# A two-layer mixer and a sparse-attention block on one NeuronCore: in the attention steps of the grouped heads, the first run of the next scores is issued between the first and the second group of turned blocks

## What is computed

```python
def block_attention(q, k, v):        # q (B,S,H,D), k (B,T,G,D), v (B,T,G,Dv)
    ...
    def one_block(qi):               # 128 queries
        s = jnp.einsum('bqgrd,bkgd->bgrqk', qi, k).astype(jnp.float32) * scale
        p = jax.nn.softmax(s, axis=-1).astype(v.dtype)
        return jnp.einsum('bgrqk,bkgv->bqgrv', p, v)
```

## Time and profile before

| | us |
|---|---|
| median of 3 runs | 4646.46 |
| the runs | 4642.58 to 4646.97 |
| span of the profiled execution | 4643.8 |
| PE busy | 4460.8 (96%) |
| DVE busy | 2440.1 (53%) |
| ACT busy | 1280.8 (28%) |

### The profile page before, as it was taken

The page is one execution under the profiler, slowest core; times in us unless marked ns, Lnnn a source line. Parts: engine busy times, 40 slices in busy tenths (PEclk is TensorE's granted clock), DMA queues, the critical chain, the costliest instruction groups (busy, mean ns, idle before and its releaser), DMA issues.

```text
span 4643.8 us, 46448 instructions
## 1 busy us (share of the span) xinstructions
PE 4460.8 (96%) x18996; PEld 2406.2 (52%) x18996; DVE 2440.1 (53%) x4042; ACT 1280.8 (28%) x2014; POOL 51.9 (1%) x74
## 2 busy tenths in 40 slices
PE   7998999999998999999999999999999999999997
PEld 3554666645444666544457645555544444444443
DVE  6677556633476566326962312333543555556554
ACT  2004444513015445223012402333300311110033
POOL 1000000000000000000000000000000000000000
PEclk9999999999999999999999999999999999999998
DMA  7212000021121000200111010000012211111111
GB/s 278 79 54 86 1 1 1 1 104 59 37 81 38 1 1 1 76 27 24 37 37 32 23 32 23 14 19 15 26 39 68 68 46 36 46 45 64 46 50 68
DMA packets 49458, 207.12 MB, mean 45 GB/s; under 512 B 4896, under 2 KB 4896, under 8 KB 46688
## 3 DMA queue, kind: packets, MB, share of 16 engines
q1 hardware_dynamic: 36512, 142.62, 9.3%
q0 software_dynamic: 12736, 61.54, 3.5%
HBM read 185.27 MB, written 18.87 MB: 44 GB/s over the span
## 4 chain that ended last, share of the span: by engine, by line
PE 91%; DVE 5%; ACT 3%; issue 1%; DMA 1%; POOL 0%; ACTq 0%; DVEq 0%; PEld 0%; PEldq 0%; SPq 0%; POOLq 0%
PE psum L2399 20%; PE psum L703 9%; PE psum L1240 7%; PE psum L1418 5%; PE psum L2079 5%; PE psum L1268 5%; PE psum L1670 5%; PE psum L1254 4%; PE psum L399 3%; PE psum L2353 3%; PE psum L1783 2%; PE psum L1773 2%; PE psum L2365 2%; PE psum L2095 2%; PE psum L1810 2%; PE psum L712 1%
## 5 line engine op out<-in xcount | busy, mean ns | idle before, releaser
L2399 PE MATMUL psum<-arena 128*128 128x512 f32 x2184 | 937.9, 592 | 0.9 <-DVEq L382 0.9
L2399 PEld LDWEIGHTS psum<-arena 128*128 128x128 f32 x2184 | 414.8, 190 | 523.2 <-issue 521.9
L703 PE MATMUL psum<-arena 128*128 128x512 f32 x952 | 410.0, 592 | 0.0
L2704 DVE TENSOR_TENSOR arena<-arena,psum 128x512 f32<-128x512 f32 x280 | 192.5, 688 | 397.1 <-PE psum L2399 388.5
L1240 PE MATMUL psum<-arena 64*128 64x512 f32 (+3 forms) x1200 | 382.9, 531 | 7.4 <-ACT arena L1195 5.8
L1337 DVE TENSOR_REDUCE arena<-psum 128x1 f32<-128x1280 f32 (+1 forms) x216 | 290.8, 1368 | 116.6 <-PE psum L1240 116.6
L1254 PE MATMUL psum<-arena 128*128 128x128 f32 x1968 | 299.9, 279 | 28.1 <-ACT arena L1311 12.8
L1254 PEld LDWEIGHTS psum<-arena 128*128 128x128 f32 x1968 | 225.9, 141 | 173.4 <-issue 110.4
L703 PEld LDWEIGHTS psum<-arena 128*128 128x128 f32 x952 | 180.9, 190 | 223.8 <-issue 222.2
L1306 ACT ACTIVATE arena<-psum,arena 128x1280 f32<-128x1280 f32 (+1 forms) x216 | 265.0, 1232 | 110.5 <-DVE arena L1337 110.4
L1311 ACT ACTIVATE arena<-psum 128x512 f32<-128x512 f32 x294 | 170.1, 596 | 327.4 <-PE psum L1254 327.2
(11 more groups left out here) (293 smaller groups left out, 5105.7 us busy)
## 6 DMA issues: line engine op xcount, KB each, us to landing
arena<-stream SPq DMA_DIRECT2D x228, 512.0 KB, 3.7
arena<-mod_t POOLq DMA_DIRECT2D x32, 512.0 KB, 4.7
arena<-mod_w POOLq DMA_DIRECT2D x4, 2048.0 KB, 26.2
arena<-stream SPq DMA_DIRECT2D x6, 1024.0 KB, 10.4
arena<-x SPq DMA_DIRECT2D x4, 1280.0 KB, 16.6
gated<-arena POOLq DMA_DIRECT2D x4, 1280.0 KB, 4.7
arena<-gated SPq DMA_DIRECT2D x1, 5120.0 KB, 15.8
arena<-x POOLq DMA_DIRECT2D x2, 2048.0 KB, 19.5
```

What stands on the lines that cost most here:

```text
L703: last = nc.tensor.matmul(ps(PROJECT_BANKS[p], 512), lhsT=lhsT(k), rhs=rhs(k), start=k == 0, stop=k == 3)
L2399: last = nc.tensor.matmul(ps(pair_bank(j, p), HALF), lhsT=lhsT(k), rhs=rhs(k), start=k == 0, stop=k == nk - 1)
L2704: step(nc.vector.tensor_tensor(out, a, b, op), ev)
```

## The change

The loop of PE's queue takes the first run of scores of the next step out of the list and issues it between group 0 and group 1, wherever `turns_first` holds; the other runs stay behind group 1.

```diff
             first = turns_first(steps, u)
-            for g in range(min(first, len(groups))):
+            if first:
+                turn(u, 0, groups[0])
+                if ahead:
+                    scores(u + 1, ahead.pop(0))
+            for g in range(1, min(first, len(groups))):
                 turn(u, g, groups[g])
             for i in range(max(len(ahead), len(groups))):
```

## The result

| | before | after |
|---|---|---|
| median, us | 4644.53 | 4656.2 |
| runs | 4642.48 to 4646.97 (7) | 4651.09 to 4660.48 (7) |
| span of the profiled execution, us | 4643.8 | 4655.3 |
| ratio to before | | 1.0023 (95%: 1.0013 to 1.0034) |

The changed kernel is slower by 0.23%: 11.7 us between the medians, 11.5 us between the profiled spans. The forecast was 4659.2 us, 12.7 us above the median of before as it stood then. A second set of runs, beside other kernels, gave 12.9 us between the medians and a ratio of 1.0031 (1.0021 to 1.0042).

A forecast was written before the change was run, and what follows sets the result against it. PE's closed gqa-step loop, with a 0.36 us hole waiting for DVE's L1358, was taken as the bound. Terms 11.2 + 0.6 + 0.1 + 0.9 = 12.8, rounded to + 12.7, on 4646.46 gave 4659.2 us; range 4648 to 4667.

The forecast's parts named there:

- The total: Whole kernel: + 12.7 us on the median of 4646.46 us, giving 4659.2 us; chance 0.74.
- What bounds the step: Gqa steps: PE's closed loop of 8.20 us, with a 0.36 us hole ahead of group 1 waiting for DVE's bank 7 reading.
- New start, + 0.04 us: Gqa steps: half 1's score waits for its exponential and starts at 806.72, 0.04 us later than group 1 did.
- Second entry, + 0.21 us: Gqa steps: scores cut in two pay one more entry (0.11 us) and exit (0.10 us) before group 2.
- The tail of 5.25 us: Gqa steps: from group 2 to the end of half 1's next exponential, 5.25 us, within a new loop of 8.45 us.
- The mla places: Layer 0: group 1 falls behind the score, 0.44 us twice, + 0.9 us; layer 1: 0, at best - 0.2 us.
- The first gqa step of layer 0: Turned blocks at half the spacing there; group 2 comes later, estimate + 0.6 us, between 0 and 1.
- The rest of the kernel should stay as it was: Outside the touched places: no change expected; a longer part elsewhere would make the sum wrong.
- No price for an entry: Rival, gqa places: PE loads the other kind's weights during the last pass; only + 3.4 us, 4649.9 us; chance 0.12.
- The hole filled after all: Rival, gqa steps: half 1's exponential ends earlier, second entry free, up to 0.36 us a step saved, 4631 us; chance 0.04.
- Half 1 waits for half 0: Rival, first score run: half 1 starts only once half 0 is through; + 0.88 us a step, 4688 us; chance 0.10.
- What would show it: Profile after: 8.45 us gqa step, first scores waiting for ACT L1306, no L1358 wait, two score-load rows with 0.54 us first passes.

The follow-up runs named there:

- x6: Kernel before, gqa places only: first two score runs issued between groups 0 and 1, the last between groups 2 and 3; ratio 0.9984 to the kernel before.

## Why the prediction was right, point by point

- **The total.** 12.7 us forecast, 11.7 measured. The prediction's own parts add up to 12.8, or to 12.6 with its 0.244 us a step, for which it gives no source; neither is 12.7.
- **What bounds the step.** Right: in the old order the hole is DVE's reading of bank 7 (7.88 us with a shorter one, 8.20 with a shorter exponential).
- **New start, + 0.04 us.** Right in kind. The exponential of half 1 ends at 805.44 + 0.21 = 805.65 and group 1 starts at 806.75, 1.10 us later; the prediction had 0.05 + 1.07 = 1.12.
- **Second entry, + 0.21 us.** Right for the stretch from the exponential to group 2: group 1 to the second entry 0.59 us, the other two runs 807.34 to 808.83 = 1.49 us, both as worked out. It is not the whole price: on PE's own loop a second entry and exit cost 0.34 us, with the slower spacing of group 0. PE's own loop of 8.22 us was seen when the exponential was made shorter.
- **The tail of 5.25 us.** 808.83 to 813.88 + 0.21 = 814.09 is 5.26 us. The sum of the step, 8.45, was 0.02 us high; 45 x 0.233 = 10.5 us instead of 11.2.
- **The mla places.** Layer 0: 0.43 us each at equal clock, as forecast; in the trace the second is 2.12 us longer, 1.69 of it from the lower clock shown above. Layer 1: 0.06 us each gained.
- **The first gqa step of layer 0.** The term that was mis-sized: 0.6 us forecast, 2.3 us measured from group 0 to group 2. The granted clock was lower there than before. The windows of that piece in after and in before (us, busy times by engine, PEclk, DMA share, GB/s):

```profile
750.40:757.80 7.40, 7.30 (x20) 3.12 (x20) 2.41 (x7) 1.44 (x3) 0.00 (x0) 0.60 0.01 2
```

```profile
747.20:752.20 5.00, 4.95 (x20) 2.98 (x20) 2.26 (x7) 1.39 (x2) 0.00 (x0) 0.66 0.01 3
```

  Both have the same 20 matmul records. In after the half clock (1.2 GHz) also covered the two other runs of scores. At full clock (1.00 granted) the piece took 4.53 us in the changed order with the shorter reading and 3.44 us in the order of before with the shorter exponential. So the order itself costs about 1.1 us here, an estimate across two kernels that differ a little, and the clock the rest. Whether the low clock belongs to the new order is not settled. The second trace of the changed kernel has it again (7.25 us from group 0 to group 2), so has the run with the gqa places alone, and a shorter stretch of it lies in the kernel before. The two shortened kernels in the changed order, at 1.00, do not have it.
- **The rest of the kernel should stay as it was.** It did not, and here luck helped. The stretch between the two layers' attention, in which nothing was changed, is 3.0 us shorter, at a higher granted clock (before, then after):

```profile
960.18:1471.83 511.65, 486.56 (x1279) 234.94 (x1276) 258.51 (x295) 112.43 (x138) 14.68 (x14) 0.98 0.20 72
971.40:1480.04 508.64, 483.52 (x1279) 233.77 (x1276) 258.47 (x295) 112.31 (x138) 14.69 (x14) 0.99 0.20 72
```

  The stretch ahead of the attention is 0.7 us longer and the one behind it 2.0 us shorter. The touched parts together grew by 15.8 us (gqa steps 10.5, the first of them 2.8, mla places 2.4, the last of layer 0 0.1), the untouched ones shrank by 4.3, which leaves the 11.5. At equal clock the touched parts come to about 12.4 us, near the 12.8 of the sum. So the mechanism and its size are shown by the traces; that the total came within 1 us is in part the half clock's moving about.
- **The rivals.** No price for an entry: fell, with the 1.49 us. The hole filled after all: fell for this order, since the exponentials did not move ahead; x6 shows that another order fills part of it. Half 1 waits for half 0: fell. In the first gqa step of layer 0 the halves can be seen apart:

```profile
751.08 0.29 PEld L1240 LDWEIGHTS psum<-arena 64*128 64x128 f32 x2 [0.17 <-issue]
...
751.89 0.50 PEld L1240 LDWEIGHTS psum<-arena 64*128 64x128 f32 x2 [0.52 <-ACT arena L1310]
```

  Half 0 loads its weights at 751.08, half 1 at 751.89, when ACT is done; in the plain steps the whole run ends 1.10 us behind the exponential, as a pair alone would.
- **What would show it.** One sign was wrong: the profile names no wait for ACT in the plain steps. The wait stands in the spread of the weight loads alone. The step (8.43), the first pass of 0.54 us behind group 1 (807.34 to 807.88) and the 1.05 us from half 1's earliest start (805.70) to group 1 came nearly as named; the first pass ahead of group 1 is hidden in the spread.

## What to carry to other kernels

A hole in the bounding engine is worth filling only if the work that is put there is free to start and if no second chain is closed by it: here two waits ended within 0.04 us of each other, and the work moved into the one hole had to wait for the other. Work out every loop that passes through the moved piece (the engine's own, and each one through a neighbour), then see which is longest in the new order; the views that name one releaser per wait show only the one that came last. And when a piece is cut into two, its entry and exit are paid twice; put the cut where another wait covers a part of it, as the order with group 2 ahead of the last run does. Last, compare pieces at the same granted clock before you put a difference down to the change.

## What the runs showed of the hardware

- At full clock, going from blocks on all 128 rows to scores on 64 rows costs 0.11 us in the first pass and 0.15 us in the group ahead of it (0.59 us, where a group takes 0.44), and leaving them 0.10 us; a second entry and exit together measured 0.34 us a step (8.22 against 7.88). The mla scores on 96 rows pay neither. By the Trainium skill, "TensorEngine Tiling (Array Packing)", section Key Properties, a change of tiling mode drains the engine; these times agree.
- Two score matmuls on different row halves are independent: the second can join 0.2 to 0.8 us late and still takes the time of a pair from its own start on (1.05 us in the plain steps; 1.05 us too in the first gqa step at full clock, where half 1 came 0.81 us late, changed order with the shorter reading). The same section says that tiles operate independently; the traces agree.
- A matmul pair of which one half waits counts as a busy engine, so that in the plain steps, where the wait is about 0.2 us, neither the waits nor the chain name what it waits for. Where half 1 came 0.81 us late, the timeline did name ACT (0.52 us).
- The granted clock of a step can differ though the code of that step and of all ahead of it is the same: the second mla place of layer 0 took 22.41 us at 1.00 in the kernel before and 24.10 us at 0.93 with the shorter exponential, which first differs in the gqa steps behind it.
